# The prologue of a two-layer decoder trunk, turned from feature tiles to token blocks

## The reference

```python
def rmsnorm(x, g):
    y = x * lax.rsqrt(jnp.mean(x * x, axis=-1, keepdims=True) + EPS)
    return y * g

# first step of the mLSTM mixer, u = rmsnorm(x, ln_mix[0])
q, k, v, o, ig, fg = jnp.split(u @ w_in, splits, axis=-1)
log_i = softcap(ig + bg[:nh], 15.0)
log_f = jax.nn.log_sigmoid(softcap(fg + bg[nh:], 15.0))
# then the chunkwise mLSTM, which needs cumulative sums and maxima of the gates
```

## Time and profile before

| what | before |
|---|---|
| median of three executions | 2455.27 us |
| span of the profiled execution, first to last instruction | 2453.2 us |
| TensorE busy | 2309.0 us, 94% of the span |
| VectorE busy | 1657.0 us, 68% |
| GpSimd busy | 921.8 us, 38% |
| ScalarE busy | 888.9 us, 36% |
| mean granted TensorE clock | 0.972 of full speed |

### The profile page before, as it was taken

The page is one execution under the profiler, slowest core; times in us unless marked ns, Lnnn a source line. Parts: engine busy times, 40 slices in busy tenths (PEclk is TensorE's granted clock), DMA queues, the critical chain, the costliest instruction groups (busy, mean ns, idle before and its releaser), DMA issues.

```text
span 2453.2 us, 28316 instructions
## 1 busy us (share of the span) xinstructions
PE 2309.0 (94%) x10601; PEld 1898.4 (77%) x10601; DVE 1657.0 (68%) x1956; ACT 888.9 (36%) x1471; POOL 921.8 (38%) x356
## 2 busy tenths in 40 slices
PE   7999997999999999998998999987999999999998
PEld 5788885777788888887777777765777788888887
DVE  7544436579939669398466666676579839669396
ACT  4131122235334243344144444444135334243345
POOL 5424336443323233231644444446442323233230
PEclk9999998999999999999999999998999999999999
DMA  6111111345271542700522222212345171442701
GB/s 175 43 35 34 43 34 52 120 154 206 69 268 58 189 172 69 269 23 34 147 58 55 52 59 60 59 36 68 112 154 206 69 274 54 187 172 69 274 1 69
DMA packets 128832, 262.61 MB, mean 107 GB/s; under 512 B 7217, under 2 KB 81122, under 8 KB 121314
## 3 DMA queue, kind: packets, MB, share of 16 engines
q1 hardware_dynamic: 122658, 243.34, 28.5%
q10 hardware_dynamic: 6080, 17.96, 3.0%
HBM read 202.56 MB, written 41.94 MB: 100 GB/s over the span
## 4 chain that ended last, share of the span: by engine, by line
PE 77%; DVE 12%; issue 3%; ACT 3%; DMA 2%; ACTq 1%; POOL 1%; DVEq 0%; SPq 0%; POOLq 0%
PE aps L865 9%; PE aps L869 9%; PE aps L867 9%; PE dps L765 5%; PE dps L767 5%; PE dps L766 5%; PE dps L869 3%; PE mps L869 3%; PE mps L865 3%; PE dps L865 3%; PE dps L867 3%; PE mps L867 3%; PE dps L747 2%; PE dps L749 2%; PE dps L748 2%
## 5 line engine op out<-in xcount | busy, mean ns | idle before, releaser
L618 POOL TENSOR_TENSOR w_hi<-w_raw,ones 128x1024 fp32r<-128x1024 f32 x64 | 164.9, 2577 | 520.2 <-PE dps L767 290.2
L765 PE MATMUL dps<-one_hi,w_hi 128*128 128x512 f32 x608 | 260.6, 429 | 12.1 <-DVE a_next L1583 12.1
L865 PE MATMUL aps<-b_ring,w_hi 128*128 128x512 f32 x640 | 252.6, 395 | 13.8 <-issue 13.8
L867 PE MATMUL aps<-b_ring,w_lo 128*128 128x512 f32 x640 | 251.7, 393 | 0.0
L869 PE MATMUL aps<-b_ring,w_hi 128*128 128x512 f32 x640 | 251.7, 393 | 0.0
L703 POOL TENSOR_TENSOR s_blk<-s_blk,a 128x1024 f32<-128x1024 f32 x32 | 93.6, 2926 | 409.0 <-DVE w_lo L1627 283.1
L767 PE MATMUL dps<-one_lo,w_hi 128*128 128x512 f32 x608 | 242.4, 399 | 0.0
L766 PE MATMUL dps<-one_hi,w_lo 128*128 128x512 f32 x608 | 241.6, 397 | 0.0
L1645 DVE TENSOR_TENSOR b_ring<-h,b_ring 128x1024 fp32r<-128x1024 f32 x120 | 222.3, 1861 | 7.5 <-ACT b_ring L1248 7.5
L622 POOL TENSOR_TENSOR w_lo<-w_raw,w_hi 128x1024 fp32r<-128x1024 f32 x64 | 160.1, 2501 | 5.0
L747 PE MATMUL dps<-one_hi,w_hi 128*128 128x512 f32 x384 | 153.4, 399 | 6.9 <-DVE m_next L1583 3.6
(11 more groups left out here) (292 smaller groups left out, 5619.1 us busy)
## 6 DMA issues: line engine op xcount, KB each, us to landing
b_ring<-xs SPq DMA_DIRECT2D x42, 2048.0 KB, 7.9
xs<-b_ring SPq DMA_DIRECT2D x14, 2048.0 KB, 7.4
a<-in_w_up SPq DMA_DIRECT2D x16, 1024.0 KB, 5.3
a<-in_w_down SPq DMA_DIRECT2D x16, 1024.0 KB, 7.5
w_raw<-in_mlstm_w_in SPq DMA_DIRECT2D x24, 512.0 KB, 4.0
w_raw<-in_diff_w_in SPq DMA_DIRECT2D x24, 512.0 KB, 3.8
hspill<-h SPq DMA_DIRECT2D x2, 4096.0 KB, 13.3
h<-hspill SPq DMA_DIRECT2D x16, 512.0 KB, 3.6
```

The lines of the kernel that those rows point to most:

```text
L618: nc.gpsimd.tensor_tensor(w_hi[:, slot], w_raw[:, slot], ones[:, :].unsqueeze(1).broadcast_to([P, NT, P]), ALU.mult).then_inc(pool_chain, 1)
L765: nc.tensor.matmul(dps[:, half], w_hi[:, slot, k], rh, start=(k == 0), stop=False)
L865: nc.tensor.matmul(to[:, n], wh, ring[:, 0, k], start=new and k == 0, stop=False, skip_group_check=not new)
L867: nc.tensor.matmul(to[:, n], wl, ring[:, 0, k], start=False, stop=False, skip_group_check=not new)
```

## The change

The prologue goes over blocks n = 0..7 of 128 tokens instead. A block is loaded as whole rows of 4 KB, 128 rows. TensorE transposes its 8 feature tiles into two PSUM banks (`x_pair`). VectorE multiplies both banks by the gain (`x_scaled_at`), one instruction of 1024 elements a partition. The copy to `h` is made by VectorE for blocks 0 and 4 (`H_FIRST`) and by ScalarE for the others. ScalarE sums the squares of a token's row straight from `x_tok`, with the sum taken along the row (`accum_out`), so that the additions on GpSimd and the column sums on TensorE are gone. ScalarE writes the high part in two instructions of 512, and VectorE the rest in two (`x_rest`), one block behind the products with the gain.

TensorE's order is now: transposes of blocks 0 to 5, the gates of tokens 0 to 511 (`gate_half(0)`, 24 matmuls), transposes of blocks 6 and 7, the first panel's first half, the gates of tokens 512 to 1023 (with the broadcast of 1/rms in its middle), the first panel's second half. VectorE takes the first half of the gates after the rest of block 7, and the second half after the norm. GpSimd's split for panel 2 now waits for the second half of the gates.

```diff
-                for d in range(start, end):
-                    sp.dma_start(x_tok[:, :, d * P:(d + 1) * P],
-                                 x_v[:, :, d * P:(d + 1) * P]).then_inc(x_ld[d], 16)
+                for n in range(start, end):
+                    sp.dma_start(x_tok[:, n], x_v[:, n]).then_inc(x_ld[n], 16)
...
-            load_x(1, 3)
+            load_x(1, 4)
...
-                    pool.wait_ge(half_done, 2 * (g - 1))
+                    pool.wait_ge(half_done, 3 if isinstance(g, int) and g == 2 else 2 * (g - 1))
...
-            for n in range(2, 2 * NT):
-                pool.wait_ge(emit_hi, n + 1)
-                if n >= 4:
-                    pool.wait_ge(x_added, n - 3)
-                nc.gpsimd.tensor_tensor(acc[:, n % 2], acc[:, n % 2], sq[:, n % 2], ALU.add).then_inc(x_added, 1)
...
+            def x_transposes(n):
+
+                if n >= 2:
+                    pe.wait_ge(x_scaled, n - 1)
+                    h_copied(pe, n - 2)
+                pe.wait_ge(x_ld[n], 16)
+                for d in range(NT):
+                    last = nc.tensor.transpose(x_pair(n)[:, d], x_tok[:, n, d * P:(d + 1) * P], ident[:, :])
+                last.then_inc(xt_done, 1)
+
+            def gate_half(half, hook=None):
+
+                pe.wait_ge(act_ready, 8 * (half + 1))
+                for d in range(NT):
+                    rh, rl = (piece(v, d, half) for v in one)
+                    nc.tensor.matmul(dps[:, half], w_hi[:, 0, d], rh, start=(d == 0), stop=False)
+                    nc.tensor.matmul(dps[:, half], w_lo[:, 0, d], rh, start=False, stop=False)
+                    last = nc.tensor.matmul(dps[:, half], w_hi[:, 0, d], rl, start=False, stop=(d == NT - 1))
+                    if hook and d == 3:
+                        hook()
+                last.then_inc(half_done, 1)
...
-            sum_squares(0)
-            half_panel(G_MIX[0], G_MIX[0] % 2, 0, *one, hook=lambda: broadcast_rstd(0))
+            x_transposes(0)
...
+            for n in range(1, 6):
+                x_transposes(n)
+            pe.wait_ge(gate_split, 1)
+            gate_half(0)
+            for n in range(6, NB):
+                x_transposes(n)
+            half_panel(G_MIX[0], G_MIX[0] % 2, 0, *one)
+            gate_half(1, hook=lambda: broadcast_rstd(0))
             half_panel(G_MIX[0], G_MIX[0] % 2, 1, *one)
...
+            for n in range(NB):
+                act.wait_ge(x_ld[n], 16)
+                if n >= 2:
+                    act.wait_ge(x_squared, n - 1)
+                nc.scalar.activation(flat(rstd_bc[:, :, :]) if n % 2 else mo[:, 1], x_tok[:, n], ACT.Square,
+                                     accum_out=small[:, 3, n:n + 1]).then_inc(x_squared, 1)
+                act.wait_ge(x_scaled, n + 1)
+                if n not in H_FIRST:
+                    nc.scalar.activation(h[:, :, n * P:(n + 1) * P], x_pair(n), ACT.Copy).then_inc(h_rest, 1)
+                for j in range(2):
+                    nc.scalar.activation(token_piece(one[0], n, j), x_scaled_at(n)[:, 4 * j:4 * j + 4],
+                                         ACT.Copy).then_inc(emit_hi, 1)
...
+            def x_rest(n):
+
+                dve.wait_ge(emit_hi, 2 * n + 2)
+                for j in range(2):
+                    nc.vector.tensor_tensor(token_piece(one[1], n, j), x_scaled_at(n)[:, 4 * j:4 * j + 4],
+                                            token_piece(one[0], n, j).bitcast(f32),
+                                            ALU.subtract).then_inc(act_ready, 1)
+
+            dve.wait_ge(gain_done, 1)
+            nc.vector.tensor_copy(gains[:, :], mps[:, 1, 0:6 * NT + 1]).then_inc(gain_ready, 1)
+            dve.wait_ge(gain_ready, 1)
+            for n in range(NB):
+                dve.wait_ge(xt_done, n + 1)
+                if n >= 3:
+                    dve.wait_ge(act_ready, 2 * (n - 2))
+                nc.vector.tensor_tensor(x_scaled_at(n), x_pair(n),
+                                        gain[:, ROW[0]].unsqueeze(2).broadcast_to([P, NT, P]),
+                                        ALU.mult).then_inc(x_scaled, 1)
+                if n in H_FIRST:
+                    nc.vector.tensor_copy(h[:, :, n * P:(n + 1) * P], x_pair(n)).then_inc(h_first, 1)
+                if n == 0:
                     dve.wait_ge(gate_ld, 32)
                     ch.link(nc.vector.tensor_copy(w_hi[:, 0], w_raw[:, 0]))
...
+                if n >= 1:
+                    x_rest(n - 1)
+            x_rest(NB - 1)
+
+            def gate_take(half):
+
+                dve.wait_ge(half_done, 2 * half + 1)
+                nc.vector.tensor_copy(g_z[0:32 + MH, half * HALF:(half + 1) * HALF],
+                                      dps[0:32 + MH, half]).then_inc(evac, 1)
+
+            gate_take(0)
+            norm(0)
+            gate_take(1)
             dve.wait_ge(evac, 2)
-            norm(0)
```

More of the change, by code:

```diff
@@ L187, in trunk, with h_copied @@
     ORDER = [(role, j, t) for role in (2, 1) for j in (1, 0) for t in range(4)]
+    H_FIRST = [0, 4]
+    def h_copied(eng, n):
+        if n in H_FIRST:
+            eng.wait_ge(h_first, H_FIRST.index(n) + 1)
+        else:
+            eng.wait_ge(h_rest, sum(j not in H_FIRST for j in range(n + 1)))
     def emitted(d, half):
@@ L377, in trunk @@
         ysplit = sem("ysplit")
[L378 removed]
+        xt_done, x_scaled, x_squared = sem("xt_done"), sem("x_scaled"), sem("x_squared")
+        h_first, h_rest = sem("h_first"), sem("h_rest")
         ss_done = sem("ss_done")
@@ L918, in out_product @@
                     panels(g + 2 * i, g % 2, 2, *one)
-            pe.wait_ge(const_ok, 4)
[L922 to L949, removed]
@@ L1151, in emit @@
                 act.wait_ge(ready, value)
-                if e == 0 and n >= 4:
-                    act.wait_ge(x_added, n - 3)
-                elif e > 0:
-                    act.wait_ge(act_ready, n - 1)
+                act.wait_ge(act_ready, n - 1)
                 src = h[:, d, cut]
-                last = nc.scalar.activation((acc if e == 0 and d == 0 else sq)[:, half], src, ACT.Square)
-                if e == 0:
-                    last = nc.scalar.activation(piece(one[0], d, half), src, ACT.Copy,
-                                                scale=gain[:, ROW[e], d:d + 1])
-                elif half == tokens(1):
+                last = nc.scalar.activation(sq[:, half], src, ACT.Square)
+                if half == tokens(1):
                     last = nc.scalar.activation(b_ring[d // 4][:, 0, d % 4], src, ACT.Copy,
@@ L1379, in mlp @@
                     down(layer, c)
-            for d in range(NT):
-                for half in range(2):
-                    emit(0, d, half, 2 * d + half, xt_copied, 2 * d + half + 1)
+            for n in range(NB):
[10 more added lines that the diff above has]
+                                         ACT.Copy).then_inc(emit_hi, 1)
             act.wait_ge(z_ready, 3)
@@ L1544, in emit @@
                 dve.wait_ge(emit_hi, n + 1)
-                if e == 0:
-                    nc.vector.scalar_tensor_tensor(piece(one[1], d, half), h[:, d, cut], gain[:, ROW[e], d:d + 1],
-                                                   piece(one[0], d, half).bitcast(f32), ALU.mult,
-                                                   ALU.subtract).then_inc(act_ready, 1)
-                    return
                 nc.vector.tensor_tensor(acc[:, half], acc[:, half], sq[:, half], ALU.add).then_inc(act_ready, 1)
@@ L1571, in norm @@
             def norm(e, sums=mps):
-                dve.wait_ge(ss_done, e + 1)
-                ch.link(nc.vector.tensor_scalar(small[:, 0], sums[:, 0, 0:NB], 1.0 / D, EPS, ALU.mult, ALU.add))
+                if e == 0:
+                    dve.wait_ge(x_squared, NB)
+                else:
+                    dve.wait_ge(ss_done, e)
+                ch.link(nc.vector.tensor_scalar(small[:, 0], small[:, 3] if e == 0 else sums[:, 0, 0:NB],
+                                                1.0 / D, EPS, ALU.mult, ALU.add))
                 rsqrt(small[:, 0], rstd[:, :], small[:, 1]).then_inc(rstd_ready, 1)
@@ L1884, in _ @@
                                             ALU.subtract).then_inc(gate_split, 1)
-                    dve.wait_ge(gain_ready, 1)
-                if s >= 1:
-                    for half in range(2):
-                        emit(0, s - 1, half, 2 * (s - 1) + half)
-            for half in range(2):
-                dve.wait_ge(half_done, half + 1)
-                last = nc.vector.tensor_copy(g_z[0:32 + MH, half * HALF:(half + 1) * HALF],
-                                             dps[0:32 + MH, half])
-                last.then_inc(evac, 1)
+                if n >= 1:
[8 more added lines that the diff above has]
+            gate_take(1)
             dve.wait_ge(evac, 2)
-            norm(0)
             def mlstm_takes(hd, start, end):
```

33 lines of the change are left out of this document (19 added, 14 removed).

## The result

The changed kernel takes 2459.91 us, the median of 17 executions (2454.77 to 2462.22), against 2455.27 of the kernel before, executed beside it (17 executions, 2450.72 to 2459.44). The ratio is 1.0016, with a 95% interval of 1.0009 to 1.0023: slower by 4.6 us, or 0.16%. The profiled execution has a span of 2459.4 us at a mean granted clock of 0.969 (before: 2453.2 and 0.972).

The account below looks back on a forecast made before the run. It took VectorE's blocks, held by GpSimd, then the gates' chain through ScalarE and VectorE to 90.63, as the bound. +8.6 to ScalarE's start and −0.6 after gave +8.0: 2463.3 us on the runs' median, range 2455.5 to 2468.5.

Parts of the forecast that it names:

- case (a): Whole kernel: the forecast itself, slower by +5 to +11 us; chance 0.52.
- three signs of being wrong: Last rest before 38, the two multiplications by 1/rms taking 1.3 together, or the take less than 5 us after 90.63.
- Part 1: Blocks up to the first gates: additions and column sums removed, one rest held by GpSimd's first split; gates begin at 26.5.
- Part 2: Last two blocks: transposes of block 6 stand behind 24 gate matmuls (7.1 us), using up the prologue's gain.
- R: The time when the last rest ends on VectorE: forecast 42.7 us, against 42.6 before.
- Part 3: Last rest to ScalarE's start: TensorE idles, panel 2's split holds the multiplications; 63.6 against 55.0, +8.6 us.
- Part 4: From ScalarE's start to the take of panel 3's second half: same work, holds shift; −0.6 us, ends −3 and +2.
- two instants that decide: When the gates reach ScalarE (55.0 before) and when VectorE gets through to the take at 90.63.
- Behind 90.63 TensorE is nearly gapless and passes the shift on: After the take of panel 3's second half: matmuls follow one another, so the summed +8.0 us carries to the end.
- Rival (b): First gates and first panel: half clock lasts through both, 24 matmuls instead of 8 in each; +12 to +15 us; chance 0.12.
- Rival (c): Rests and multiplications by 1/rms: GpSimd hardly holds them up; +2 to +4.9 us; chance 0.24.
- Rival (d): Maxima: splits for panels 4 and 5 leave them, the 10.8 us of holds vanish; −2 or −6 us; chance 0.12.

Follow-up runs that it names:

- transposes_first: Changed kernel with transposes of blocks 6 and 7 ahead of the first half of the gates on TensorE; −1.1 us against the kernel before, ratio 0.9999.
- before_no_adds: Kernel before without GpSimd's 14 additions of squares and the waits for them, leaving out part of the computation; −8.5 us against the kernel before, ratio 0.9963.
- take_early: Changed kernel with VectorE's take of the first half of the gates ahead of its product 6; −1.9 us against the kernel before, ratio 0.9991.
- split2_later: Changed kernel with GpSimd's split for panel 2 held until both gate halves are multiplied by 1/rms; +7.3 us against the kernel before, ratio 1.0028.
- all_together: Changed kernel with block 6's transposes, the gates' take and small work earlier, splits for panels 2 and 5 held; 2444.62 us, ratio 0.9958 to the kernel before.
- row_squares_only: Kernel before with GpSimd's additions replaced by ScalarE's sums of squares along token rows; −2.9 us against the kernel before, ratio 0.9989.
- small_work_early: Changed kernel with VectorE's small work in its broadcast wait and panel 2's split held until the multiplications end; ratio 1.0008 to the kernel before.
- after_again: Changed kernel executed and profiled again with no edit, as control; 2459.98 us against 2455.48 for the kernel before, ratio 1.0016.

## Why the prediction was right, and where its size was off

The forecast was slower by 8.0 us (0.33%); it became slower by 4.6 (0.16%). That lies inside the stated range of 2455.5 to 2468.5, but it is less than the case (a) forecast for itself, +5 to +11, and within the 0.2% to which the prediction gave 0.29. None of its three signs of being wrong came: the last rest ended at 41.3 and not before 38, the multiplications took 5.04, and the take came 6.15 us later. Step by step:

- **Part 1, first gates at 26.5.** 24.7. The first split ran at 12.90, not 14.3, and held one pair of rests to 18.7. The mechanism stands, with 1.8 us less.
- **Part 2, first gates 7.1, transposes of block 6 at 34.7, R at 42.7.** 7.9 (some twelve matmuls at half clock and not eight), the product with block 6 at 33.65, R = 41.3. "The prologue's gain is used up here" is what transposes_first shows: without that order the last rest ends at 35.2, and before_no_adds ends it at 34.7.
- **Part 3, TensorE idle some 7 us; ScalarE's start at 63.6.** 7.5 idle, and 63.33, which is +8.3 against the +8.6 forecast. That this fits within 0.3 is partly luck: R came 1.4 us early, and the stretch from R took 22.0 instead of 20.9 (twelve matmuls at half clock again, and 5.04 for the multiplications). take_early and transposes_first each remove nearly all of the idle stretch, and 9 to 10 us at the marker with it (6.5 and 5.7 in the medians).
- **Part 4, −0.6 from there to the take near 99.** This is the term that was mis-sized. The take came at 96.78, so the stretch gave back 2.2 of the 8.3. Held instructions cost 8.0 us above their usual (2.05, 2.18, 2.44 and 3.46, where 0.47, 0.15, 0.28 and 1.22 are usual). Before, five had cost 11.6, counted with the 2.62 of unheld scans (the prediction had 10.8). So 3.6 are saved, 2.9 of them on the scans, which the split for panel 3 now leaves free, as forecast. What was to be paid back for it was 1.6, for small work held by that split. It held none: the clearings took 0.91 each and the takes 0.68 beside it. Paid back were 1.4, by VectorE's waits for TensorE at the takes at 74.50 and 79.87 (0.42 and 0.96), which it hadn't there before.
- **The path in Part 4.** The prediction named two instants that decide, and the first, ScalarE's start, wasn't on the path any more. TensorE stood for 3.3 us until the take of panel 1 at 66.34, and panel 2 then set when the maxima could go on. split2_later shows it: with ScalarE 5 us earlier the last take stayed. It was a near thing, since the way through ScalarE was shorter by the same 1.4 us only, and so the forecast of the take was off by no more than the term above.
- **"Behind 90.63 TensorE is nearly gapless and passes the shift on."** Not quite: +6.15 at the take became +4.55 at the marker. Before, the seven us behind its take ran at a granted clock of 0.76 (0.43 us a matmul at 94.41); after, at 1.00. That is 22 matmuls against 28 in the two windows of seven us, and about the 1.6 us that are missing. It is what two single profiles show, and no run settles it.

So 0.3 up to ScalarE's start, 2.2 − 0.6 = 1.6 in Part 4 and 1.6 behind it make up the 3.4 between forecast and result.

One reading of the rows was wrong, without harm to the sum: the instruction at 46.37 wasn't held until the GpSimd instruction of 43.75 was over, which was at 46.10, but until the next instruction of that split was over (46.19 to 48.57).

Rival (b) needed half clock through both batches of matmuls; it lasted for some twelve in each, and the marker says no. Rival (c), GpSimd hardly holding up the multiplications or the rests, gave +2 to +4.9 and so the measured time, but by a mechanism that isn't there: the multiplications took 5.04, a pair of rests 4.50. Rival (d), the splits for panels 4 and 5 leaving the maxima, didn't come true: they began at 79.92 and 90.80, each beside two of the maxima's instructions. It is worth pointing out what the prediction had right without using it: it said that the second half of the change (the order) eats what the first half (the additions) wins, and didn't price how much a better order is worth. before_no_adds puts the first at 8 us, and all_together puts the second at some 15, with the splits and the small work.

What stays open: in two of the three groups the medians lie 2.3 to 4.4 us above what the marker says (transposes_first −5.3 and −1.1; row_squares_only −7.3 and −2.9), in the other within 1. The executions of one kernel lie up to 5 us on either side of their median, but for the one at 4122.89. The profiles show where a lead goes: in that of transposes_first it is still 5.1 us at the attention part's first GpSimd product (1176.9 against 1182.0), and 1.5 at the last one (1628.6 against 1630.1); in that of row_squares_only 5.5 and 2.2, of all_together 11.9 and 8.5. The changed kernel's lag stays near 5 over the same stretch. The code there is the same in all of them; no run ties the loss to a cause.

## What to carry to other kernels

Price a faster stage by the queue behind it, on each in-order engine: here a take that stood behind the last rest and two transposes that stood behind 24 matmuls gave back all of an 8 us gain and more. Then read again which engine the chain goes through behind the changed stage, since it may have moved. When the sum of squares leaves GpSimd, that alone is worth trying before the loop is rebuilt around it. And when GpSimd holds up a VectorE instruction with two SBUF operands, look which such instruction is next in the queue before the split is moved: the hold moves to it, however small it is.

## What the runs showed of the hardware

- A hold lasts until GpSimd's instruction beside it is over, however small VectorE's is: products of 64 elements a partition took 2.32 and 2.43 us (split2_later) where they take 0.22, and a scan of 128 elements on four partitions 2.63 (small_work_early) for 0.48. About one such VectorE instruction gets through for each of GpSimd's: the two multiplications of 5.04 took 2.25 and 2.87, beside the two instructions of one split (2.38 and 2.72).
- The two MEMSETs of 1024 elements took 0.91 each at 64.35 and 65.42 of the changed kernel, while GpSimd's split ran from 63.91 to 68.7: they were not held. The Trainium skill (GPSIMD Engine Reference, Specifications) names only instructions in a two-port mode or with two SBUF inputs as contending; these rows agree. L1982, a subtraction of a scalar in SBUF from one SBUF tensor, was held for 2.44 at 90.84; whether it runs in a two-port mode no run shows.
- How long a batch of matmuls stays at half clock differs: some twelve matmuls at 24.7 and at 42.0 in the changed kernel, the first after 1.7 and the second after 7.5 us without a matmul; seven in take_early after the same 1.7; three where the transposes ran straight before it (transposes_first). after_again had a mean of 0.73 instead of 0.69 for the same first gates.
